# Three squared-ReLU feed-forwards of a two-block model: the next stage's input parts formed between the last evictions, squares folded on GpSimd, and a shorter interleave of column steps

## Chip, cores and metric

One core of a Trainium2 chip (trn2) runs the whole program. The metric is the device time of one execution in microseconds (us). Before the change the median of three runs is 1051.44 us (1051.43 to 1052.15). The engines are TensorE (PE; PEld is its weight load), VectorE (DVE), ScalarE (ACT), GpSimd (POOL) and SyncE (SP), which issues the weight transfers.

## The reference

256 tokens of width 1024 pass through two models in fp32. The first is a pooling and gated-delta-rule mixer followed by a feed-forward; the second is a spatial-gating mixer, a feed-forward, an RWKV-7 mixer and a feed-forward. What matters here is the feed-forward, which stands there three times (FFN1, FFN2, FFN3), and the norm in front of each stage:

```python
def rms_norm(x, w):
    return x * lax.rsqrt(jnp.mean(x * x, axis=-1, keepdims=True) + EPS) * w

h = h + jnp.square(jax.nn.relu(u @ w_up)) @ w_down      # u = rms_norm(h, norm_mlp), w_up 1024x4096, w_down 4096x1024
```

After FFN1 come the first model's final norm, the second model's first norm and the gating mixer (the kernel's `sgu` stage, whose first product is `h @ w_in`, 1024x4096). After FFN2 comes the RWKV mixer, whose first products are small low-rank ones. After FFN3 comes the final norm.

## The kernel before

**Layout.** The residual `x` stays in SBUF as 8 tiles of 128 channels by 256 tokens. Each fp32 matrix is multiplied as a high and a low part, both in the matmul's fast fp32r type. Weights come in 1 MB units (128x2048). SP loads a unit into one of four `raw` buffers, ACT copies it to `w_high` (`high`, L671), and DVE subtracts to get `w_low` (`low`, L1228). A load waits until the `low` of the unit four before it is done.

**Activations.** They are split in the same way: ACT writes `x` times the norm's channel weight to the high part, DVE writes the rest to the low part (L1493 before a feed-forward, L1520 `gating_low` before the gating stage, L1530 `mixer_low` before the RWKV stage). The norm's per-token factor is applied after the product. It needs the sum of squares of `x`: ACT squares all 8 tiles (L867), `halved` on DVE adds the tiles up in three steps of 1024, 512 and 256 columns (L1512, L1514), and one matmul with ones sums over channels (L2497).

**A feed-forward** (`mlp`) is 32 units m = 0 to 31, in four groups of 8: four units of `w_up`, then four of `w_down`. A unit is 16 column steps (2 tiles of 128 outputs by 8 slices k of the contraction), each of one 512-column matmul with the high weight (L2445) and one 256-column matmul with the low weight (L2446). Three pairs of PSUM banks are used in turn. An up unit is evicted by ACT (`copy_half`, L883), by a DVE add (L1550) and a DVE squared ReLU (L1556), and is then split by ACT (`hidden_high`, L889) and DVE (`hidden_low`, L1563). A down unit is evicted by ACT L883 and DVE L1550, L1570 and L1575, which adds it to two tiles of `x`. In each group the first two down units are interleaved, since their slices k = 6, 7 come from the fourth up unit: 12 column steps of unit m0+4, 12 of unit m0+5, then the 4 and 4 that are left. The last unit, m = 31, uses three 256-column matmuls a step (L2082 to L2084). Its first tile is released to DVE half a unit before its second (`last_tile`), and L1609 and L1611 add both to tiles 6 and 7 of `x`.

**Order around the change.** Each engine runs its list strictly in order, and the lists are written out by hand.

- On DVE, step m of the loop is: eviction of unit m, `low` of unit m+3, and `hidden_low` for an up unit. After the loop (m = 30) DVE runs `after_sum(0)` to `after_sum(2)`, that is the low parts of tiles 0 to 5 for the next stage, then L1609 and L1611 for tiles 6 and 7, then `after_sum(3)`. In FFN1 `after_sum` is `gating_low`, in FFN2 `mixer_low`, and in FFN3 nothing.
- On ACT the next stage's high parts (L909, L958), and its squares (L910, L960), stand behind the whole loop. In the RWKV stage `high` of unit `U_RKV+2` stands behind those.
- On PE the gating stage's first unit uses tiles 0 to 3 of the parts only, the second unit tiles 4 to 7. The RWKV stage starts with the sums over the squares of tiles 0 to 3, the small products of tile 0, the sums over tiles 4 to 7 (L2592), and the small products of tiles 1 to 7.
- GpSimd has little to do: three-step sums in the first mixer (L627, L630), a mask, and parts of the RWKV inputs (L644, L649).

## Time and profile before

| | |
|---|---|
| median of three runs | 1051.44 us (1051.43 to 1052.15) |
| the profiled execution | 1051.24 us, its span 1049.4 us |
| TensorE clock granted | 0.997 of full speed |
| PE busy | 1027.1 us (98%) |
| DVE busy | 823.9 us (79%) |
| ACT busy | 557.9 us (53%) |
| POOL busy | 32.6 us (3%) |
| DMA | 167 MB, 159 GB/s over the span |

The span is what the profile's rows cover; 1.8 us of the profiled execution's time lies around it. FFN1 runs from 127 to 308 us of the span, FFN2 from 459 to 639 us and FFN3 from 856 to 1039 us. A busy share is an average over the whole; what decides a stage is which wait of its bounding engine ends last there.

### The profile page before, as it was taken

Reading aid. Unit: us, or ns where it says so; the run is one execution under the profiler, and the core shown is the slowest. Engines: PE = TensorE matmul, PEld = TensorE weight load, DVE = VectorE, ACT = ScalarE, POOL = GpSimd, SP = SyncE. Lnnn points to the kernel's source line nnn. Section 1 sums busy time; section 2 is a strip of 40 time slices with the busy share of each in tenths; the row PEclk is TensorE's granted clock in tenths of the full one; section 3 lists DMA queues with packets and bytes.
Section 4 is the critical chain, followed back from the end, with each engine's and each line's share of the span. In section 5 each row is a group of like instructions: output and inputs, shape, how many; then the busy total and the mean of one; then the engine's idle time right before and its main releaser. Section 6 shows DMA issues by size and latency. Waiting matters only on the chain.

```text
span 1049.4 us, 17837 instructions
## 1 busy us (share of the span) xinstructions
PE 1027.1 (98%) x7496; PEld 928.3 (88%) x7496; DVE 823.9 (79%) x1176; ACT 557.9 (53%) x684; POOL 32.6 (3%) x39
## 2 busy tenths in 40 slices
PE   7999999999999999999999999999999999999997
PEld 7999988888887899998888888999898998888886
DVE  6989698687777787678979768799978667868775
ACT  6847554544536465355555446797553254544441
POOL 0004000000000000000000000042000000000000
PEclk9999999999999999999999999999999999999999
DMA  9722475565954755564656565414200157547531
GB/s 290 228 82 81 161 218 184 161 214 166 340 163 144 218 164 207 160 188 131 218 155 225 162 199 161 141 62 152 70 2 2 45 177 221 193 139 230 165 117 41
DMA packets 155936, 167.23 MB, mean 159 GB/s; under 512 B 5840, under 2 KB 148816, under 8 KB 155472
## 3 DMA queue, kind: packets, MB, share of 16 engines
q1 hardware_dynamic: 154672, 165.92, 49.9%
q8 instruction: 59, 0.97, 0.4%
q10 hardware_dynamic: 1184, 0.17, 0.2%
q14 instruction: 21, 0.17, 0.0%
HBM read 165.03 MB, written 1.05 MB: 158 GB/s over the span
## 4 chain that ended last, share of the span: by engine, by line
PE 79%; DVE 13%; ACT 3%; issue 2%; SPq 1%; DMA 1%; DVEq 0%; ACTq 0%
PE banks L2445 31%; PE banks L2446 16%; PE banks L2082 8%; PE banks L2084 7%; PE banks L2083 7%; DVE sb_w_low L1228 3%; DVE sb_arena L1915 1%; DVE sb_state L1912 1%; DMA sb_raw<-in_w_in 1%; ACT sb_w_high L671 1%; PE banks L2563 1%; SPq L550 1%; DVE sb_arena L1550 1%; PE banks L2696 0%; DVE sb_arena L1570 0%
## 5 line engine op out<-in xcount | busy, mean ns | idle before, releaser
L1228 DVE TENSOR_TENSOR sb_w_low<-sb_raw,sb_w_high 128x2048 fp32r<-128x2048 f32 x148 | 337.6, 2285 | 32.6 <-ACT sb_w_high L671 32.5
L671 ACT ACTIVATE sb_w_high<-sb_raw 128x2048 fp32r<-128x2048 f32 x148 | 281.8, 1908 | 12.3 <-PE banks L2084 10.2
L2445 PE MATMUL banks<-sb_act_parts,sb_w_high 128*128 128x512 f32 x768 | 270.6, 394 | 0.5 <-DVE sb_act_parts L1493 0.4
L2446 PE MATMUL banks<-sb_act_parts,sb_w_low 128*128 128x256 f32 x768 | 214.5, 279 | 0.0
L883 ACT ACTIVATE sb_arena<-banks 128x512 f32<-128x512 f32 x93 | 55.5, 597 | 243.7 <-PE banks L2446 243.7
L2445 PEld LDWEIGHTS banks<-sb_act_parts,sb_w_high 128*128 128x128 f32 x768 | 143.9, 187 | 36.1 <-DVE sb_act_parts L1493 0.7
L2082 PE MATMUL banks<-sb_act_parts,sb_w_low 128*128 128x256 f32 x584 | 169.3, 290 | 0.8 <-DVE sb_arena L1788 0.7
L2084 PE MATMUL banks<-sb_act_parts,sb_w_high 128*128 128x256 f32 x584 | 165.0, 282 | 0.0
L2083 PE MATMUL banks<-sb_act_parts,sb_w_high 128*128 128x256 f32 x584 | 164.0, 281 | 0.0
L1550 DVE TENSOR_TENSOR sb_arena<-sb_arena,banks 128x512 f32<-128x512 f32 x93 | 63.6, 684 | 102.4 <-ACT sb_arena L883 102.3
L2446 PEld LDWEIGHTS banks<-sb_act_parts,sb_w_low 128*128 128x128 f32 x768 | 144.0, 187 | 0.0
L2445 PE MATMUL banks<-sb_hidden_slots,sb_w_high 128*128 128x512 f32 x360 | 130.9, 395 | 1.3 <-DVE sb_hidden_slot L1563 1.3
L2445 PE MATMUL banks<-sb_hidden_slot,sb_w_high 128*128 128x512 f32 x360 | 130.2, 394 | 0.0
L2082 PEld LDWEIGHTS banks<-sb_act_parts,sb_w_low 128*128 128x128 f32 x584 | 109.9, 188 | 2.8 <-DVE sb_arena L1788 0.9
L2083 PEld LDWEIGHTS banks<-sb_act_parts,sb_w_high 128*128 128x128 f32 x584 | 110.7, 190 | 0.5 <-issue 0.2
L2084 PEld LDWEIGHTS banks<-sb_act_parts,sb_w_high 128*128 128x128 f32 x584 | 109.4, 187 | 0.0
L2446 PE MATMUL banks<-sb_hidden_slots,sb_w_low 128*128 128x256 f32 x360 | 100.9, 280 | 0.0
L2446 PE MATMUL banks<-sb_hidden_slot,sb_w_low 128*128 128x256 f32 x360 | 100.8, 280 | 0.0
L2445 PEld LDWEIGHTS banks<-sb_hidden_slots,sb_w_high 128*128 128x128 f32 x360 | 67.6, 188 | 18.6 <-DVE sb_w_low L1228 1.7
L2445 PEld LDWEIGHTS banks<-sb_hidden_slot,sb_w_high 128*128 128x128 f32 x360 | 67.5, 187 | 16.0
L2446 PEld LDWEIGHTS banks<-sb_hidden_slots,sb_w_low 128*128 128x128 f32 x360 | 67.5, 188 | 0.0
L2446 PEld LDWEIGHTS banks<-sb_hidden_slot,sb_w_low 128*128 128x128 f32 x360 | 67.5, 188 | 0.0
(469 smaller groups left out, 1530.7 us busy)
## 6 DMA issues: line engine op xcount, KB each, us to landing
sb_raw<-in_ffn_w SPq DMA_DIRECT2D x64, 1024.0 KB, 5.4
sb_raw<-in_w_up SPq DMA_DIRECT2D x16, 1024.0 KB, 5.5
sb_raw<-in_w_down SPq DMA_DIRECT2D x16, 1024.0 KB, 5.2
sb_raw<-in_sgu_w_in SPq DMA_DIRECT2D x16, 1024.0 KB, 5.6
sb_raw<-in_rwkv_w_rkv SPq DMA_DIRECT2D x12, 1024.0 KB, 5.2
sb_raw<-in_w_in SPq DMA_DIRECT2D x8, 1024.0 KB, 9.6
sb_raw<-in_sgu_w_out SPq DMA_DIRECT2D x8, 1024.0 KB, 5.0
sb_raw<-in_w_out SPq DMA_DIRECT2D x4, 1024.0 KB, 5.1
```

Of the source, the lines that this page charges most:

```text
L550: sp.dma_start(half_of(raw[j], t), w_in_v[:, :, c * 256 + t * P:c * 256 + t * P + P])\
L671: nc.scalar.activation(whi[s][:], raw[s][:], ACT.Copy).then_inc(hi_done, 1)
L883: nc.scalar.activation(dst, halves_at(FFN_BANK(m))[:, :, 1, :], ACT.Copy).then_inc(half_copied, 1)
L1228: nc.vector.tensor_tensor(wlo[s][:], raw[s][:], f32(whi[s][:]), ALU.subtract).then_inc(lo_done, 1)
L1550: nc.vector.tensor_tensor(t, t, halves_at(FFN_BANK(m))[:, :, 0, :], ALU.add).then_inc(unit_taken, 1)
L1912: base.add(nc.vector.tensor_tensor(tmp, RW.LB[:, j + 1:, j:j + 1].broadcast_to(shape), RW.WB[:, j:j + 1, 0:j + 1].broadcast_to(shape), ALU ...
L1915: base.add(nc.vector.tensor_tensor(RW.WB[:, j + 1:, 0:j + 1], RW.WB[:, j + 1:, 0:j + 1], tmp, ALU.add))
L2082: nc.tensor.matmul(dst, l_lo, r_hi, start=start, stop=False, **kw)
L2083: nc.tensor.matmul(dst, l_hi, r_lo, start=False, stop=False, **kw)
L2084: return nc.tensor.matmul(dst, l_hi, r_hi, start=False, stop=stop, **kw)
L2445: nc.tensor.matmul(two(dst), l_hi, parts, start=start, stop=False, skip_group_check=True)
L2446: return nc.tensor.matmul(dst[:, T:2 * T], l_lo, parts[:, 0, :], start=False, stop=stop, skip_group_check=True)
```

## The change

1. **GpSimd folds the squares.** `halved` on DVE is taken out of each feed-forward. A new function on GpSimd, `fold_squares`, does the same three additions and signals the same semaphore.
2. **The next stage's parts move into the loop.** On ACT `next_high(0)` stands behind `copy_half(29)`, `next_high(1)` behind `high` of step 29, `next_high(2)` and `(3)` behind step 30. On DVE `after_sum(0)` stands behind the eviction of unit 29. Behind the loop FFN1 has `after_sum(1)`, `(2)`, the last unit's tiles, `after_sum(3)`, and only then `low` of the gating stage's second unit (`u0+33`), which used to stand ahead of all of them. FFN2 has that `low`, the last tiles, and then `after_sum(1)` to `(3)`. In FFN2 ACT's `high(U_RKV+2)` stands ahead of the last two squares, and these are two operations of one tile each.
3. **Interleave.** Of the first two down units the order is now 12 steps of m0+4, 6 of m0+5, the last 4 of m0+4, 6 of m0+5, the last 4 of m0+5. For the fourth up unit of a group DVE runs `hidden_low` ahead of `low`.
4. **PE.** The RWKV stage's sums over tiles 4 and 5 stand ahead of the first small products. The gating stage's first matmul waits for `unit_taken`.

```diff
@@ -630,10 +630,22 @@
                     pool.wait_ge(box_sum, g + 1)
+        def fold_squares(j):
+            pool.wait_ge(sq_done, SQ[("ffn1", "ffn2", "ffn3")[j]] + 1)
+            for n in (4, 2):
+                chain.add(pool.tensor_tensor(FB.sq[:, 0:n, :], FB.sq[:, 0:n, :], FB.sq[:, n:2 * n, :], ALU.add))
+                chain.settle()
+            pool.tensor_tensor(FB.ss[j], FB.sq[:, 0, :], FB.sq[:, 1, :], ALU.add).then_inc(sq_folded, 1)
+        if on["ffn1"]:
+            fold_squares(0)
         if on["sgu"]:
...
             pool.memset(SG.ws[64:P, :, 0:64], 0.0).then_inc(mask_done, 1)
+        if on["ffn2"]:
+            fold_squares(1)
         if on["rwkv"]:
@@ -650,6 +662,8 @@
             pool.memset(RW.W6[0:32, :, 32:64], 0.0).then_inc(w_corner, 1)
+        if on["end"]:
+            fold_squares(2)
     @block.scalar
@@ -845,7 +859,7 @@
             high(U_OUT + 5)
-        def mlp(j):
+        def mlp(j, next_high=lambda c: None):
             u0, xd, h0 = FFN_U[j], FFN_X[j], FFN_H[j]
@@ -890,6 +904,8 @@
                 copy_half(m)
+                if m == len(FFN_ORDER) - 3:
+                    next_high(0)
                 if m + 4 < len(FFN_ORDER) or (m + 4 < len(FFN_ORDER) + 2 and u0 + m + 4 < n_units):
@@ -898,15 +914,42 @@
                     nc.scalar.activation(la_hi[n][:], RW.la_sc[n], ACT.Copy).then_inc(la_hi_done, 1)
+                if m == len(FFN_ORDER) - 3:
+                    next_high(1)
+            next_high(2)
+            next_high(3)
+        def gating_high(c):
+            act.wait_ge(g_done, 1)
+            act.wait_ge(x_done, X_FFN1 + c + 1)
+            for k in (2 * c, 2 * c + 1):
+                nc.scalar.activation(act_hi[:, k, :], x[:, k, :], ACT.Copy, scale=SG.g[:, k:k + 1]).then_inc(a_hi, 1)
+        def mixer_high(c):
+            def parts():
+                for k in (2 * c, 2 * c + 1):
+                    nc.scalar.activation(h_hi2[:, k, 1:T + 1], x[:, k, :], ACT.Copy, scale=vcol("norm_mix_g1", k))\
+                        .then_inc(a_hi, 1)
+            if c < 3:
+                act.wait_ge(x_done, X_FFN2 + c + 1)
+                parts()
+                nc.scalar.activation(RW.sq[:, 2 * c:2 * c + 2, :], x[:, 2 * c:2 * c + 2, :], ACT.Square)\
+                    .then_inc(sq_done, 1)
+                return
+            high(U_RKV + 2)
+            act.wait_ge(x_tile, 2)
+            nc.scalar.activation(RW.sq[:, 6, :], x[:, 6, :], ACT.Square)
+            act.wait_ge(x_done, X_FFN2 + 4)
+            nc.scalar.activation(RW.sq[:, 7, :], x[:, 7, :], ACT.Square).then_inc(sq_done, 1)
+            parts()
         if on["ffn1"]:
-            mlp(0)
+            mlp(0, gating_high if on["sgu"] else lambda c: None)
         if on["sgu"]:
-            act.wait_ge(g_done, 1)
-            for k in range(KT):
-                act.wait_ge(x_done, X_FFN1 + k // 2 + 1)
-                nc.scalar.activation(act_hi[:, k, :], x[:, k, :], ACT.Copy, scale=SG.g[:, k:k + 1]).then_inc(a_hi, 1)
             nc.scalar.activation(SG.sq[0][:], x[:], ACT.Square).then_inc(sq_done, 1)
@@ -950,15 +993,8 @@
         if on["ffn2"]:
-            mlp(1)
+            mlp(1, mixer_high if on["rwkv"] else lambda c: None)
         if on["rwkv"]:
-            for c in range(4):
-                act.wait_ge(x_done, X_FFN2 + c + 1)
-                for k in (2 * c, 2 * c + 1):
-                    nc.scalar.activation(h_hi2[:, k, 1:T + 1], x[:, k, :], ACT.Copy, scale=vcol("norm_mix_g1", k))\
-                        .then_inc(a_hi, 1)
-                nc.scalar.activation(RW.sq[:, 2 * c:2 * c + 2, :], x[:, 2 * c:2 * c + 2, :], ACT.Square).then_inc(sq_done, 1)
-            high(U_RKV + 2)
             act.wait_ge(ss_done, SS["rwkv"] + 1)
@@ -1534,8 +1570,6 @@
             low(u0 + 3)
-            dve.wait_ge(sq_done, SQ[("ffn1", "ffn2", "ffn3")[j]] + 1)
-            halved(FB.sq, FB.ss[j]).then_inc(sq_folded, 1)
             def token_scale():
@@ -1579,10 +1613,14 @@
                     down_taken(m)
-                u = u0 + m + 3
-                if m and (m + 3 < len(FFN_ORDER) or (m + 3 < len(FFN_ORDER) + 2 and u < n_units)):
-                    low(u)
-                if FFN_ORDER[m][0] == "up":
+                up_last = FFN_ORDER[m][0] == "up" and m % 8 == 3
+                if up_last:
+                    hidden_low(m)
+                if m == len(FFN_ORDER) - 3:
+                    after_sum(0)
+                if m and (m + 3 < len(FFN_ORDER) or (m + 3 == len(FFN_ORDER) and u0 + m + 3 < n_units)):
+                    low(u0 + m + 3)
+                if FFN_ORDER[m][0] == "up" and not up_last:
                     hidden_low(m)
@@ -1594,23 +1632,36 @@
                             .then_inc(la_lo_done, 1)
-            for c in range(3):
-                after_sum(c)
             t, b = FB.t[j][1], FFN_BANK(len(FFN_ORDER) - 1)
-            dve.wait_ge(x_added, 12 * j + 12)
-            dve.wait_ge(x_done, FFN_XO[j] + 2)
-            for i in range(2):
-                if i:
-                    dve.wait_ge(w_used, u0 + len(FFN_ORDER))
-                else:
-                    dve.wait_ge(last_tile, j + 1)
-                chain.add(nc.vector.tensor_tensor(t[:, i, :], tiles_at(b)[:, i, :], FB.r2[j], ALU.mult))
-                chain.settle()
-                nc.vector.tensor_tensor(x[:, 6 + i, :], x[:, 6 + i, :], t[:, i, :], ALU.add)\
-                    .then_inc(x_done if i else x_tile, 1)
-            after_sum(3)
+            def last_taken():
+                dve.wait_ge(x_added, 12 * j + 12)
+                dve.wait_ge(x_done, FFN_XO[j] + 2)
+                for i in range(2):
+                    if i:
+                        dve.wait_ge(w_used, u0 + len(FFN_ORDER))
+                    else:
+                        dve.wait_ge(last_tile, j + 1)
+                    chain.add(nc.vector.tensor_tensor(t[:, i, :], tiles_at(b)[:, i, :], FB.r2[j], ALU.mult))
+                    chain.settle()
+                    nc.vector.tensor_tensor(x[:, 6 + i, :], x[:, 6 + i, :], t[:, i, :], ALU.add)\
+                        .then_inc(x_done if i else x_tile, 1)
+            u = u0 + len(FFN_ORDER) + 1
+            if j == 1 and u < n_units:
+                low(u)
+                last_taken()
+                after_sum(1)
+                after_sum(2)
+                after_sum(3)
+            else:
+                after_sum(1)
+                after_sum(2)
+                last_taken()
+                after_sum(3)
+                if u < n_units:
+                    low(u)
         def scale_lora(n):
@@ -2468,17 +2519,16 @@
                 return FB.slots[k // 2][:, :, k % 2, :]
-            def down(m, ks=range(KT)):
+            def down(m, t, ks):
                 q = FFN_ORDER[m][1]
...
                 pe.wait_ge(h_lo, h0 + 4 * q + ks[-1] // 2 + 1)
-                for t in range(2):
-                    for k in ks:
-                        cs = slice(t * P, t * P + P)
-                        ins = wide(bank[FFN_BANK(m) + t], h[:, k, cs], l[:, k, cs], hidden_of(q, k),
-                                   start=k == 0, stop=k == KT - 1)
-                if ks[-1] == KT - 1:
-                    ins.then_inc(w_used, 1)
+                for k in ks:
+                    cs = slice(t * P, t * P + P)
+                    ins = wide(bank[FFN_BANK(m) + t], h[:, k, cs], l[:, k, cs], hidden_of(q, k), start=k == 0,
+                               stop=k == KT - 1)
+                return ins
             def down_last(m):
@@ -2495,13 +2545,19 @@
                     nc.tensor.matmul(bank[6][:, 0:T], ones, FB.ss[j], start=True, stop=True).then_inc(ss_done, 1)
-                down(m0 + 4, range(6))
-                down(m0 + 5, range(6))
-                down(m0 + 4, range(6, KT))
-                down(m0 + 5, range(6, KT))
-                down(m0 + 6)
+                down(m0 + 4, 0, range(6))
+                down(m0 + 4, 1, range(6))
+                down(m0 + 5, 0, range(6))
+                down(m0 + 4, 0, range(6, KT))
+                down(m0 + 4, 1, range(6, KT)).then_inc(w_used, 1)
+                down(m0 + 5, 1, range(6))
+                down(m0 + 5, 0, range(6, KT))
+                down(m0 + 5, 1, range(6, KT)).then_inc(w_used, 1)
+                down(m0 + 6, 0, range(KT))
+                down(m0 + 6, 1, range(KT)).then_inc(w_used, 1)
                 if m0 + 7 < len(FFN_ORDER) - 1:
-                    down(m0 + 7)
+                    down(m0 + 7, 0, range(KT))
+                    down(m0 + 7, 1, range(KT)).then_inc(w_used, 1)
                 else:
@@ -2540,6 +2596,8 @@
                         if g == 0 and m == 0:
+                            if k == 0:
+                                pe.wait_ge(unit_taken, 31)
                             pe.wait_ge(a_lo, A_SGU + k + 1)
@@ -2605,11 +2663,11 @@
             input_sums(1)
+            input_sums(2)
             pe.wait_ge(la_lo_done, 2)
...
             small_products(0)
-            input_sums(2)
             input_sums(3).then_inc(ss_done, 1)
...
```

## Rows read from the trace of the kernel before

**Rows 1.** The page's chain of work that ended last: shares of the span by engine.

```profile
PE 79%; DVE 13%; ACT 3%; issue 2%; SPq 1%; DMA 1%; DVEq 0%; ACTq 0%
```

**Rows 2.** Waits of PE: line, releaser, us in total, times, longest.

```profile
PE banks L2592 <- ACT sb_over_act L960: 2.4, 1, 2.4
...
PE banks L2082 <- DVE sb_act_parts L1520: 1.5, 1, 1.5
...
PE banks L2445 <- DVE sb_hidden_slot L1563: 1.3, 1, 1.3
```

**Rows 3.** FFN2 as one stretch: us, busy us of PE, PEld, DVE, ACT, POOL; clock, DMA.

```profile
458.70:639.50 180.80, 180.80 (x1045) 157.88 (x1044) 146.98 (x147) 95.23 (x94) 0.00 (x0) 1.00 0.58 181
```

**Rows 4.** Timeline, end of FFN1 (start, us, engine, line, operation, idle before).

```profile
307.49 0.28 PE L2084 MATMUL banks<-sb_hidden_slot,sb_w_high 128*128 128x256 f32 x1
...
309.31 0.47 PE L2082 MATMUL banks<-sb_w_high,sb_act_parts 128*128 128x512 f32 x1 [1.54 <-DVE sb_act_parts L1520]
...
306.48 2.28 DVE L1228 TENSOR_TENSOR sb_w_low<-sb_raw,sb_w_high 128x2048 fp32r<-128x2048 f32 x1
...
308.68 2.45 DVE L1520 SCALAR_TENSOR_TENSOR sb_act_parts<-sb_x,sb_gating_norms,sb_act_parts 128x256 fp32r<-128x256 f32 x6
...
312.30 0.42 DVE L1611 TENSOR_TENSOR sb_x<-sb_x,sb_arena 128x256 f32<-128x256 f32 x1
...
312.76 0.91 ACT L909 ACTIVATE sb_act_parts<-sb_x,sb_gating_norms 128x256 fp32r<-128x256 f32 x2 [5.25 <-DVE sb_x L1611]
```

**Rows 5.** Timeline, end of FFN2, sums and squares of the RWKV input.

```profile
639.37 1.89 PE L2592 MATMUL banks<-sb_over_act,sb_ones 128*128 128x256 f32 x8
...
642.61 1.03 PE L2592 MATMUL banks<-sb_over_act,sb_ones 128*128 128x256 f32 x4
...
646.04 1.18 PE L2592 MATMUL banks<-sb_over_act,sb_ones 128*128 128x256 f32 x4 [2.40 <-ACT sb_over_act L960]
...
638.25 2.29 DVE L1228 TENSOR_TENSOR sb_w_low<-sb_raw,sb_w_high 128x2048 fp32r<-128x2048 f32 x1
...
644.10 0.43 DVE L1611 TENSOR_TENSOR sb_x<-sb_x,sb_arena 128x256 f32<-128x256 f32 x1
...
645.37 0.61 ACT L960 ACTIVATE sb_over_act<-sb_x 128x512 f32<-128x512 f32 x1
```

**Rows 6.** Timeline, start of FFN3, to the first down unit.

```profile
862.30 1.90 ACT L867 ACTIVATE sb_arena<-sb_x 128x2048 f32<-128x2048 f32 x1
...
866.03 2.29 DVE L1228 TENSOR_TENSOR sb_w_low<-sb_raw,sb_w_high 128x2048 fp32r<-128x2048 f32 x1 [0.91 <-ACT sb_w_high L671]
...
868.24 1.94 DVE L1512 TENSOR_TENSOR sb_arena<-sb_arena 128x1024 f32<-128x1024 f32 x2
...
870.22 0.43 DVE L1514 TENSOR_TENSOR sb_arena<-sb_arena 128x256 f32<-128x256 f32 x1
...
880.93 0.68 DVE L1563 TENSOR_TENSOR sb_hidden_slot<-sb_arena,sb_hidden_slot 128x512 fp32r<-128x512 f32 x1
...
881.76 0.47 PE L2445 MATMUL banks<-sb_hidden_slots,sb_w_high 128*128 128x512 f32 x1 [1.29 <-DVE sb_hidden_slot L1563]
```

**Rows 7.** Timeline, the same place in FFN1: last hidden part, first down matmul.

```profile
149.34 0.69 DVE L1563 TENSOR_TENSOR sb_hidden_slot<-sb_arena,sb_hidden_slot 128x512 fp32r<-128x512 f32 x1
...
150.18 0.47 PE L2445 MATMUL banks<-sb_hidden_slots,sb_w_high 128*128 128x512 f32 x1
```

**Rows 8.** Timeline, GpSimd beside DVE in the first mixer.

```profile
82.83 2.28 DVE L1228 TENSOR_TENSOR sb_w_low<-sb_raw,sb_w_high 128x2048 fp32r<-128x2048 f32 x1
...
82.99 2.60 POOL L630 TENSOR_TENSOR sb_arena<-sb_arena 128x256 f32<-128x256 f32 x1 [44.13 <-DVE sb_arena L1279]
...
85.66 0.64 POOL L627 TENSOR_TENSOR sb_arena<-sb_arena 128x271 f32<-128x271 f32 x1
...
90.83 0.94 POOL L630 TENSOR_TENSOR sb_arena<-sb_arena 128x256 f32<-128x256 f32 x1
...
91.33 0.99 DVE L1447 TENSOR_TENSOR sb_keys_by_token<-sb_arena,sb_keys_by_token 128x512 f32<-128x512 f32 x1
```

## The prediction, made before the changed kernel was run

> **What bounds the kernel now.** I read the chain of work that ended last first: 79% of it is matmuls, 13% DVE [rows 1]. So only time in which PE stands still can be won. The list of what PE waited for comes next. Apart from the program's start it has three entries over 1 us, and each touches a feed-forward: squares from ACT (L2592), gating parts from DVE (L1520), a hidden part from DVE (L1563) [rows 2]. Third I read one feed-forward as a stretch: FFN2 takes 180.8 us, all of it PE-busy, with DVE busy 147.0 and ACT 95.2 [rows 3]. A unit is therefore 180.8/32 = 5.65 us and one of its 16 column steps about 0.35 us. Inside a feed-forward nothing is to be won on PE, but DVE has only about 1 us to spare per unit, which matters below. Last come the timelines around the three waits.
>
> End of FFN1 [rows 4]: PE's last matmul starts at 307.49 and its next at 309.31. Matmuls of this kind follow each other every 0.12 us, so 1.7 us is lost (the row's 1.54 counts from a modelled end). The cause is the order on DVE. The `low` of the second gating unit, which PE needs a whole unit later, runs from 306.48 to 308.76, and the low parts of tiles 0 to 5 only start at 308.68. PE's row starts as the first of them ends.
>
> End of FFN2 [rows 5]: PE does four sums from 639.37, the small products of tile 0, two more sums from 642.61, and then idles 2.40 us until the squares of tiles 6 and 7. DVE has again a `low` first (638.25 to 640.54), then the six low parts, and takes the last tile only at 644.53. ACT's two high parts stand ahead of its square (645.37 to 645.98). Four sums took 1.7 us (eight matmuls, 1.89 less the tail of the last), so two take 0.87. The loss from start to start is 646.04 - 642.61 - 0.87 = 2.6 us.
>
> Start of FFN3 [rows 6]: the first down unit waits 1.3 us (start to start 1.5) for `hidden_low` of the third up unit, 880.93 to 881.61. Before it DVE has hardly paused since the fold of the squares (868.24 to 870.65). In FFN1 the same part ends at 150.03 and PE starts at 150.18 [rows 7]: just in time, no loss.
>
> **The change part by part.**
>
> *FFN1's end.* The low parts of tiles 0 and 1 now come right behind unit 29, tiles 2 to 5 behind unit 30. Let E be the end of FFN1 on PE. Unit 28 ends at E - 14.7 (5.6 + 5.6 + 10 steps of 0.35), unit 29 at E - 11.2, unit 30 at E - 5.6. An eviction is ACT's copy (0.6, as a 128x512 operation [rows 5]) and three DVE operations (each about 0.7, as the hidden part [rows 6]). DVE's list from E - 13.9 on is: eviction (2.1), `low` (2.2), eviction of unit 29 (to E - 7.5), two low parts (0.8, from 2.45/6 each [rows 4]), `low` (to E - 4.5), eviction of unit 30 (to E - 2.4), four low parts (to about E - 0.9, the last two behind ACT). The gating stage's first unit uses tiles 0 to 3 alone, so PE goes on at once: -1.7 us. Its new wait, `unit_taken`, was met at about E - 3.8. What is late next is `low` of the second unit, which moved to the very end. From E DVE does L1609 and L1611 (0.85), waits for ACT's two high parts (0.9 [rows 4]; DVE's first starts halfway), does two low parts (ending about E + 2.4), then `low` (2.28): E + 4.7. PE needs it one unit after E: 24 matmuls of 512 columns, 0.23 each by the part of a column step beyond the 256-column one (0.35 - 0.12), so E + 5.6. It is covered with 0.9 us to spare; without that cover it would cost its own length, 2.3. Behind it in DVE's queue stand a fold of squares (2.4) and the third unit's `low` (2.3), done by E + 9.4 and needed at E + 11.2. On SP the load of the unit four later waits for the moved `low`, some 4 us later than now, and its `high` comes only after the first gating group: no cost.
>
> *FFN2's end.* By the same count unit 30 is evicted at E - 2.4. DVE does `low` of the second RKV unit until about E - 0.2 and takes the last two tiles by E + 1.4. ACT does two parts and a square (1.5), then `high` of the third RKV unit (1.9, as its 128x2048 square [rows 6]) until about E + 1.0, so the square of tile 7 (about 0.5) ends near E + 1.9. PE covers that with six sums (2.6) and the small products of tile 0 (642.61 - 639.37 - 1.73 = 1.5): it reaches the last sums at E + 4.1. The whole gap goes: -2.6 us; I count 2.5. The remaining low parts are done by E + 3.8, and PE needs tile 2 only after E + 5. The norm's factor is ready sooner as well, since ACT's `high` is no longer in front of it.
>
> *The fold on GpSimd.* DVE is rid of 2.4 us per feed-forward (1.94 and 0.43) [rows 6]. The same additions on GpSimd: one over 271 columns with no DVE operation of two SBUF inputs beside it takes 0.64 us [rows 8]; scaled to 1024 + 512 + 256 columns that is 4.3 us, less if part of the 0.64 is fixed. The sum is needed at 880, and the squares are ready at 864.20, so its own length is covered by 11 us. But GpSimd and DVE get in each other's way. A GpSimd addition of 256 columns that started beside `low` (82.83 to 85.11) ended at 85.59, 2.60 us instead of about 0.64. In turn a DVE operation of 128x512 (normally 0.69, as the hidden part) took 0.99 beside GpSimd [rows 8]. One waits while the other has the inputs.
>
> So in FFN3: GpSimd starts when `low` of unit 2 ends (about 865.1) and holds to about 867.4. `low` of unit 3, ready at 866.03, ends near 869.6 instead of 868.32. GpSimd's second addition holds to 870.7; the eviction's add reads PSUM and passes, but the squared ReLU waits and ends at 871.3 instead of 871.97. DVE is earlier by about 0.7 us and not by 2.4. The bounds are 1.5 (no hindrance: the whole stall goes) and -1.9 (every microsecond of the 4.3 held against DVE: 2.4 - 4.3). I take 0.8, near the walk-through. In FFN1 and FFN2 there is no stall to remove. DVE has there 0.1 us of margin at that point, and the same walk gives a DVE between equal and 1 us earlier: 0.
>
> The Trainium skill, SBUF — State Buffer, section "SBUF: two separate sides", states a lock between a GpSimd operation and a DVE operation with two SBUF inputs, held for the whole instruction. By that rule a 1024-column addition blocks `low` for all its length, as in my walk, and the sum stays; if short holds were shared instead, FFN3 would gain 1.5 and the sum 0.7 more. Rows 8 agree with the rule for 256 columns, and no row shows a longer addition on GpSimd.
>
> *Interleave.* The hidden part of the fourth up unit is now needed after 18 steps instead of 24: 6.3 us instead of 8.4 after that unit. It comes after copy, `high` and `hidden_high` on ACT (0.6 + 1.9 + 0.6, by the same rows) and 0.7 on DVE: 3.8 us. Margin 2.5; cost 0. `low` moved behind it ends at about 6.1 and is needed at 11.2. The first down unit finishes 6 steps (2.1 us) earlier, which spreads the evictions; PE wins nothing.
>
> *Sum.* -1.7 - 2.5 - 0.8 = -5.0 us. The profiled execution, 1051.24 with a span of 1049.4, would become 1046.2 with a span of 1044.4. It lies 0.2 below the median of the runs, so against the median I forecast 1046.4. Everything behind each gap waits on PE or on work released by it, and moves along.
>
> **The rivals.**
>
> - *The fold is free for DVE* (GpSimd alone waits): FFN3's 1.5 us go whole, 1051.44 - 5.7 = 1045.7. For it: `low` at 82.83 took its normal 2.28. Against it: the 0.99 of L1447.
> - *Gap 1 comes back one unit later*: if DVE is over 0.9 us later than I walked it, the moved `low` holds PE at the second gating unit. With 1.5 lost there: about 1047.9.
> - *The fold doesn't free DVE*: GpSimd blocks it for all 4.3 us. DVE is 1.9 later in each of three places with 0.1 us of margin, 1.8 + 1.8 + 1.9 = 5.5 against 1.7 + 2.5 won: 1052.7 at the worst, near 1051 with half of it hidden in DVE's pauses. The change then does nothing to be seen.
> - *Slower: GpSimd is slow for real.* If 2.60 us for 256 columns is its own pace and no waiting, the fold takes 7 times that, 18.2 us. PE's ones matmul then waits in each feed-forward. In FFN3, 864.2 + 18.2 = 882.4 and up to 2.3 for the `low` ahead of it, against a start at 880.3; in the other two it is about 3.5 late too. That is 3.5 + 3.5 + 4.4 - 1.5 (the stall that is there already) = about 10 lost against 4.2 won, near 1057. PE begins to wait once a fold takes over 14 us (880.3 - 864.2 - 2.3), and the change loses from about 15.5 us on. Against it: 0.64 us three microseconds later.
>
> **How the numbers follow.** Forecast 1046.4: chance 0.52. Free fold 1045.7: 0.22. Moved `low` 1047.9: 0.12. Fold doesn't free DVE: 0.08. Slow GpSimd: 0.06. What a measurement of this kernel can tell is about 0.2%, 2.1 us, so "faster" means below 1049.3. The first three cases are faster: 0.86. The fourth is mostly within: 0.07, the rest of it and the last case slower: 0.07. The range's low end takes the free fold and 0.8 us for a shorter RWKV start: 1044.8. The high end takes the moved `low` together with no gain in FFN3: 1048.9. That leaves out about 2 in 10.
>
> **What would show it.** PE's wait for L1520 and for ACT's square (L960) gone from its list; at FFN1's end the moved `low` ending about 4.7 us after PE's last FFN1 matmul; a wait of under 1 us left for the hidden part in FFN3; GpSimd additions of about 2.3, 1.2 and 0.6 us plus waiting, and a `low` of over 3 us beside the first. I am wrong if PE waits at the gating stage's second unit, if new waits on L1563 show up in FFN1 or FFN2, or if the ones matmul waits for GpSimd.

## The result, and the profile after

The changed kernel takes 1044.03 us (median of 4 runs, 1043.7 to 1044.1) where the kernel before takes 1051.43 beside it: a ratio of 0.9935 [0.992, 0.9951], which is 6.8 us less by the ratio and 7.4 us less by the medians. A second comparison gave 1044.34 (1044.27 to 1045.42, 5 runs) and 0.9933 [0.992, 0.9946]. The forecast was 1046.4 with a low end of 1044.8: the sign was right, but 5.0 us were forecast, some 2 us too few, and the result lies 0.8 us outside the range. The runs of one kernel lie in groups (26 runs of the kernel before: 5 at 1049.5 to 1049.9, 15 at 1050.8 to 1051.4, 6 at 1052.3 to 1053.4); what makes them is part of the answer below.

The page of the changed kernel, its chain of work that ended last (span 1042.2 us, execution 1044.1), answers to [rows 1]; the list of what PE waited for (line, releaser, us in total, times, longest) answers to [rows 2]; FFN2 as a stretch answers to [rows 3] (us; busy us of PE, PEld, DVE, ACT, POOL; granted clock; DMA).

```profile
PE 83%; DVE 11%; ACT 3%; issue 2%; SPq 1%; DMA 1%; DVEq 0%; ACTq 0%
```

```profile
PE banks L2242 <- DMA sb_x<-in_x_t: 5.5, 1, 5.5
PE banks L2133 <- DVE sb_arena L1839: 0.7, 1, 0.7
PE banks L2958 <- DVE sb_arena L1968: 0.6, 1, 0.6
PE banks L2496 <- DVE sb_hidden_slot L1597: 0.6, 1, 0.6
```

```profile
456.70:637.50 180.80, 180.80 (x1046) 158.09 (x1045) 149.11 (x150) 96.75 (x95) 7.01 (x3) 1.00 0.58 181
```

Apart from the program's start no wait over 0.7 us is left. The squares (2.4) and the gating parts (1.5) are gone, and the hidden part went from 1.3 to 0.6. FFN2 takes as long as before, to 0.2 us (180.8 us in both stretches).

The end of FFN1, which answers to [rows 4] (start, us, engine, line, operation, idle before):

```profile
307.28 0.28 PE L2135 MATMUL banks<-sb_hidden_slot,sb_w_high 128*128 128x256 f32 x1
...
307.40 0.40 PE L2133 MATMUL banks<-sb_w_high,sb_act_parts 128*128 128x512 f32 x1
...
309.19 0.88 DVE L1556 SCALAR_TENSOR_TENSOR sb_act_parts<-sb_x,sb_gating_norms,sb_act_parts 128x256 fp32r<-128x256 f32 x2 [0.71 <-ACT sb_act_parts L927]
...
309.99 2.28 DVE L1264 TENSOR_TENSOR sb_w_low<-sb_raw,sb_w_high 128x2048 fp32r<-128x2048 f32 x1
```

PE goes on after 0.12 us where it took 1.82 (start to start). The moved `low` ends at 312.27, which is 4.9 us after PE's start of 307.40.

The end of FFN2, which answers to [rows 5]:

```profile
637.16 2.75 PE L2650 MATMUL banks<-sb_over_act,sb_ones 128*128 128x256 f32 x12
...
638.61 0.42 ACT L946 ACTIVATE sb_over_act<-sb_x 128x256 f32<-128x256 f32 x1 [0.25 <-DVE sb_x L1648]
...
641.19 1.03 PE L2650 MATMUL banks<-sb_over_act,sb_ones 128*128 128x256 f32 x4
641.84 0.19 PEld L2133 LDWEIGHTS banks<-sb_mixer_input_high,sb_lora_low 128*128 128x128 f32 x1
641.87 0.47 PE L2133 MATMUL banks<-sb_mixer_input_high,sb_lora_low 128*128 128x256 f32 x1
```

The last square is done at 639.03, 2.2 us before PE wants it. From the first sum to the second tile's small products PE takes 4.71 us instead of 7.45 (646.82 - 639.37): -2.74.

The start of FFN3, which answers to [rows 6]:

```profile
857.57 6.42 POOL L637 TENSOR_TENSOR sb_arena<-sb_arena 128x1024 f32<-128x1024 f32 x2 [116.62 <-ACT sb_arena L881]
864.07 1.07 POOL L639 TENSOR_TENSOR sb_arena<-sb_arena 128x256 f32<-128x256 f32 x1
...
859.33 3.50 DVE L1264 TENSOR_TENSOR sb_w_low<-sb_raw,sb_w_high 128x2048 fp32r<-128x2048 f32 x1 [0.92 <-ACT sb_w_high L685]
...
863.46 1.07 DVE L1590 SCALAR_TENSOR_TENSOR sb_arena<-sb_arena 128x512 f32<-128x512 f32 x1
...
873.50 0.68 DVE L1597 TENSOR_TENSOR sb_hidden_slot<-sb_arena,sb_hidden_slot 128x512 fp32r<-128x512 f32 x1
...
874.33 0.48 PE L2496 MATMUL banks<-sb_hidden_slots,sb_w_high 128*128 128x512 f32 x1 [0.56 <-DVE sb_hidden_slot L1597]
```

The `low` beside GpSimd's first addition takes 3.50 us instead of 2.28 (the prediction walked 3.6), and PE's wait shrinks by 0.73 us start to start.

**Where the time went.** I compared when the same matmul (by its number in PE's list) starts in the two traces. Over the profiled pair the gain is 7.24 us at FFN3's last matmul: 0.21 by the end of FFN1, 1.70 at that end, 0.10 in the gating stage, 0.20 in FFN2, 2.74 at its end, **1.51 in the stretch of the RWKV stage from the second tile's small products to the decay product** (17.55 to 16.04 us), 0.25 in the rest of RWKV, 0.73 at FFN3's first down unit, less 0.20 given back behind it. The 1.51 is in none of my terms. The trace of before has its cause, in rows that I had not read. PE goes on at 646.04, behind the 2.40 us pause of [rows 5]. First its timeline a little later, then three stretches (same columns as above; the last but two is the granted clock):

```profile
647.65 0.41 PE L2082 MATMUL banks<-sb_mixer_input_high,sb_lora_low 128*128 128x256 f32 x1
647.86 0.41 PE L2083 MATMUL banks<-sb_mixer_input_low,sb_lora_high 128*128 128x256 f32 x1
...
650.79 0.28 PE L2083 MATMUL banks<-sb_mixer_input_low,sb_lora_high 128*128 128x256 f32 x1
650.90 0.28 PE L2084 MATMUL banks<-sb_mixer_input_high,sb_lora_high 128*128 128x256 f32 x1
```

```profile
646.04:647.00 0.96, 0.96 (x5) 0.86 (x5) 0.01 (x1) 0.96 (x1) 0.00 (x0) 1.00 1.10 350
646.80:650.40 3.60, 3.60 (x18) 3.57 (x17) 1.76 (x6) 3.54 (x6) 0.00 (x0) 0.53 1.10 349
650.50:654.10 3.60, 3.60 (x32) 3.60 (x31) 3.60 (x10) 3.60 (x8) 0.00 (x0) 1.00 0.21 66
```

and the same place in the changed kernel:

```profile
642.00:645.60 3.60, 3.60 (x32) 3.57 (x31) 2.37 (x7) 3.28 (x6) 0.00 (x0) 1.00 1.05 292
```

Behind the pause PE runs for 0.96 us more at the full clock (2.4 GHz), and then for about 3.4 us at the lower one (1.2 GHz): 16 matmuls of 256 columns start 0.213 us apart instead of 0.118, which costs 16 x 0.095 = 1.5 us. PE counts as fully busy in that time, so neither its busy share nor a list of waits shows it.

The Trainium skill, TensorE: Matmul & The Clock Gate, section "HAM oscillation — how this bites in real kernels", says that pauses between groups of matmuls let the clock fall, so that the next group starts at the lower one. The trace of before agrees that the clock falls behind a pause (0.53 against 1.00). It differs in two points, and there the trace decides: the fall comes 0.96 us after the next group has started, and the pause of 2.40 us is shorter than the waits for DMA in the page's example.

### The profile page after: what moved, and what is told of

It reads as the page before. It is cut to its first block, busy times and chain, and to the rows that moved or that the text cites. A ratio compares the mean times of both kernels' runs of the same rounds, so it can differ in the third digit from the quotient of the medians.

```text
span 1042.2 us, 17910 instructions
## 1 busy us (share of the span) xinstructions
PE 1025.3 (98%) x7496; PEld 927.8 (89%) x7496; DVE 824.7 (79%) x1167; ACT 558.9 (54%) x685; POOL 54.9 (5%) x48
## 4 chain that ended last, share of the span: by engine, by line
PE 83%; DVE 11%; ACT 3%; issue 2%; SPq 1%; DMA 1%; DVEq 0%; ACTq 0%
PE banks L2496 32%; PE banks L2497 16%; PE banks L2133 8%; PE banks L2135 8%; PE banks L2134 8%; DVE sb_w_low L1264 2%; DVE sb_arena L1966 1%; DVE sb_state L1963 1%; DMA sb_raw<-in_w_in 1%; ACT sb_w_high L685 1%; PE banks L2754 1%; PE banks L2621 1%; SPq L550 1%; PE banks L2865 0%; DVE sb_arena L1432 0%
## 5 line engine op out<-in xcount | busy, mean ns | idle before, releaser
L1264 DVE TENSOR_TENSOR sb_w_low<-sb_raw,sb_w_high 128x2048 fp32r<-128x2048 f32 x148 | 341.3, 2310 | 33.1 <-ACT sb_w_high L685 33.1
```

The costliest lines, as they stand in the source:

```text
L1264: nc.vector.tensor_tensor(wlo[s][:], raw[s][:], f32(whi[s][:]), ALU.subtract).then_inc(lo_done, 1)
```

## The experiments

**1. Is the missing 1.5 us the clock?** To the kernel before I add five ones matmuls, whose result nobody uses, in the pause. The last sums still wait for the same square.

```diff
             input_sums(2)
+            for _ in range(5):
+                nc.tensor.matmul(bank[7][:, 0:T], ones, RW.sq[:, 0, :], start=True, stop=True)
             input_sums(3).then_inc(ss_done, 1)
```

> The kernel before with five more ones matmuls into an unused bank between the sums over tiles 4 and 5 and the last sums, so PE is busy for 2.15 of the 2.6 us that it otherwise stands still; what it waits for comes no sooner. The results of these matmuls are not used. Theory (the pause drops the clock): the half clock is gone and 1.5 us are won although the wait's end stays. Rival (the rest of the gain at this place comes from the norm's factor and ACT's high being earlier): no change, within 0.2 us.

Measured: 1049.62 us (1049.17 to 1051.01, 10 runs), 0.9988 [0.9979, 0.9997]. PE's timeline:

```profile
644.37 2.32 PE L2614 MATMUL banks<-sb_over_act,sb_ones 128*128 128x256 f32 x10
646.92 1.13 PE L2592 MATMUL banks<-sb_over_act,sb_ones 128*128 128x256 f32 x4 [0.24 <-ACT sb_over_act L960]
```

```profile
646.90:650.50 3.60, 3.58 (x26) 3.47 (x27) 1.01 (x5) 3.55 (x4) 0.00 (x0) 1.00 1.10 346
```

The square comes no sooner, yet the stretch from the first sum to the decay product takes 23.50 us instead of 25.00. With PE kept busy the clock stays at 1.00 and the 1.5 us come back. So they hang on PE standing still, and come on top of the time for which it does.

**2. Does the pause always cost them?** Two ways: the kernel before once more, unchanged, and the changed kernel with a pause of the old size put back (11 squares of tile 7 that are not needed, ahead of the real one).

> The kernel before once more, for a second profile. Its timed runs lie in groups near 1049.6, 1051.1 and 1052.5 us. Theory: two things vary from execution to execution, the start (FFN1's first matmul at 127 or at 128.5 us) and the half clock behind the pause at FFN2's end (3.4 us of it or none), each worth 1.3 to 1.5 us; the profile shows which two this execution had, and they add up to its time. Rival: the groups come from elsewhere, and the stretch from FFN2's end to the decay products is 25.0 us as before without a half clock.

```diff
             act.wait_ge(x_done, X_FFN2 + 4)
+            for _ in range(11):
+                chain.add(nc.scalar.activation(RW.sq[:, 7, :], x[:, 7, :], ACT.Square))
+                chain.settle()
             nc.scalar.activation(RW.sq[:, 7, :], x[:, 7, :], ACT.Square).then_inc(sq_done, 1)
```

> The changed kernel with 11 needless squares of tile 7 on ACT ahead of the one that PE waits for, each about 0.47 us: PE stands still again for about 2 to 3 us at FFN2's end. Theory (a pause of this length drops the clock): the half clock comes back for 3.4 us behind the pause, and the stretch from FFN2's end to the RWKV stage's decay products is longer by the pause plus 1.5 us. Rival (the half clock of before had another cause): longer by the pause alone.

> The kernel with the late square once more, for a second profile. In its first profile PE stood still for 2.8 us and the clock stayed at full speed, though the timed runs lie at 1047.2 once, at 1048.5 to 1048.9 six times and at 1049.8 to 1050.1 three times. Theory (such a pause drops the clock in most executions, not in all): this profile shows either no half clock and about 1047.1 us, or 3.4 us of half clock behind the pause and about 1048.6 us. Rival (the pause has nothing to do with it): no half clock whatever the time; the 1.4 us between the groups then lie at the start alone.

Measured: before again 1049.91 us in its profiled execution, with the same 2.40 us wait and no drop; the stretch takes 23.50 us. Changed with the pause: 1048.73 us (1047.15 to 1050.13, 10 runs), 0.9981 [0.9972, 0.999]. Its profiled execution (1047.15) has no drop, a second one (1050.05) has. The stretch behind the pause in before again, then behind a pause of 2.67 and of 2.66 us in the other two:

```profile
646.80:650.40 3.60, 3.60 (x31) 3.55 (x30) 1.59 (x6) 3.54 (x5) 0.00 (x0) 1.00 1.10 352
```

```profile
645.00:648.40 3.40, 3.40 (x30) 3.38 (x29) 2.59 (x9) 2.96 (x5) 0.00 (x0) 1.00 1.10 348
```

```profile
646.80:650.20 3.40, 3.40 (x18) 3.40 (x17) 2.59 (x9) 3.34 (x7) 0.00 (x0) 0.50 1.10 349
```

The same pause costs 1.5 us in one execution and nothing in the next. The 1050.05 is made up of 1047.15, a start of FFN1 that is 1.3 us later, and 1.5 for the clock. The same pause stands in the traces of experiments 4 and 7 (FFN1's end alone, the fold alone), and both have the drop: four traces of six with the pause in all. This also explains the groups: FFN1's first matmul starts at 126.9 to 127.5 us in eight traces and at 128.0 to 128.7 in the other eight, whatever the kernel, and a run with the pause may or may not have the drop.

The mean granted clock that is listed for each run tells how often. In the 16 traces it is 0.997 or less where the drop is there and 0.998 or more where it is not. Of the kernel before's 26 runs 20 have 0.997 or less. The other six are the whole lowest group and one run of the middle group (1051.02), which fits a late start without the drop. In its four comparisons together the kernel before has the drop in 42 of 57 runs, the changed kernel with the pause in 9 of 11. The 38 runs of kernels without the pause and the ten with the filled one all have 0.998 or 0.999. The seven faster runs of the filled kernel (1049.17 to 1049.79) lie where the kernel before's lowest group does. The changed kernel has only the groups of the start (1044.3 and 1045.4 in its second comparison).

**3. FFN2's end alone** (the kernel before, with the parts of the change that touch it):

```diff
+            if j == 1:
+                low(u0 + len(FFN_ORDER) + 1)
+                last_taken()
+                after_sum(1)
...
+            input_sums(2)
...
             small_products(0)
-            input_sums(2)
             input_sums(3).then_inc(ss_done, 1)
```

> The kernel before with only FFN2's end changed (parts and squares in the loop, ACT's high of the third RKV unit ahead of the last two squares, the sums over tiles 4 and 5 ahead of the small products). Theory: this edit takes away PE's 2.40 us wait and with it the 3.4 us at half clock (1.2 GHz instead of 2.4) that the trace of before shows right behind that wait, in which 16 matmuls ran at 0.213 us each instead of 0.118: 2.7 + 1.5 = about 4.2 us won. Rival, the prediction's own term: the wait alone, 2.5 to 2.7 us won, and the rest of the 7.4 us comes from elsewhere.

Measured: 1048.16 (1047.06 to 1048.62, 5 runs), 0.9968 [0.9955, 0.9981]. Between the first sum and the decay product the profiled execution gains 2.61 + 1.51 = 4.12 us, with no drop of the clock:

```profile
644.40:648.00 3.60, 3.60 (x28) 3.43 (x27) 3.33 (x10) 3.12 (x7) 0.00 (x0) 1.00 1.06 297
```

The 4.2 stands; a gain of the pause alone falls. In a run of the kernel before that has no drop, only the 2.6 are there to be won.

**4. FFN1's end alone:**

```diff
+            if j == 0:
+                after_sum(1)
+                after_sum(2)
+                last_taken()
+                after_sum(3)
+                low(u0 + len(FFN_ORDER) + 1)
```

> The kernel before with only FFN1's end changed. Theory: 1.7 us won, the distance of the two matmuls beyond their step; no half clock there before, so nothing beyond it. Rival: part of the unexplained 2.4 us is here (the gating stage's folds start earlier against PE), 2.5 us or more won.

Measured: 1050.52 (1048.91 to 1051.89, 10 runs), 0.9995 [0.9986, 1.0004]: no gain clear of the noise. The trace has the 1.70 us won at the first gating matmul and 1.19 lost behind it, nearly all one unit later, so 0.5 is left. DVE's parts and `low`, then PE at the gating stage's second unit:

```profile
311.06 0.88 DVE L1529 SCALAR_TENSOR_TENSOR sb_act_parts<-sb_x,sb_gating_norms,sb_act_parts 128x256 fp32r<-128x256 f32 x2 [0.71 <-ACT sb_act_parts L913]
311.86 2.28 DVE L1237 TENSOR_TENSOR sb_w_low<-sb_raw,sb_w_high 128x2048 fp32r<-128x2048 f32 x1
314.20 0.50 PE L2104 MATMUL banks<-sb_w_high,sb_act_parts 128*128 128x512 f32 x1 [1.00 <-DVE sb_w_low L1237]
```

DVE is 1.9 us later here than in the changed kernel (311.86 against 309.99, at the same start of the gating stage). Theory and rival of the expectation both missed this: the part depends on another one.

**5. Which one? The changed kernel with the old interleave:**

```diff
                 down(m0 + 5, 0, range(6))
+                down(m0 + 5, 1, range(6))
                 down(m0 + 4, 0, range(6, KT))
                 down(m0 + 4, 1, range(6, KT)).then_inc(w_used, 1)
-                down(m0 + 5, 1, range(6))
```

> The changed kernel with the old interleave of the first two down units (12, 12, 4 and 4 column steps). Theory, from the run with FFN1's end alone: unit 28 ends 2.1 us later, DVE's row of evictions, parts and lows at FFN1's end moves back by about 1.3 us, and PE waits 1.2 us for the moved low at the gating stage's second unit; nothing elsewhere. Rival, the prediction's own term: the interleave costs and gains nothing, 0.

Measured: 1047.0 (1045.73 to 1047.63, 6 runs), 0.9964 [0.9951, 0.9976]. The wait is back, 1.15 us at the gating stage's second unit. The rest of the profiled execution loses another 0.3 us in small steps. DVE's row and PE's:

```profile
313.59 2.28 DVE L1264 TENSOR_TENSOR sb_w_low<-sb_raw,sb_w_high 128x2048 fp32r<-128x2048 f32 x1
315.93 0.50 PE L2133 MATMUL banks<-sb_w_high,sb_act_parts 128*128 128x512 f32 x1 [1.00 <-DVE sb_w_low L1264]
```

The interleave releases unit 28 six steps sooner, DVE's row at FFN1's end moves up, and the moved `low` comes in time. It is worth 1.2 us at this place, beside the moved `low`. The interleave without the other parts was not run, so its worth alone is not shown. This run keeps `hidden_low` ahead of `low` for the fourth up unit; that half of part 3 was not run apart either.

**6. FFN1 with FFN2's order on DVE** (`low` ahead of the last tiles and of `after_sum(1)`):

```diff
-            if j == 1 and u < n_units:
+            if j < 2 and u < n_units:
                 low(u)
```

> The changed kernel, in FFN1 with FFN2's order on DVE behind the loop: low of the next stage's second unit and the last tiles ahead of the low parts of tiles 2 to 7. Theory (PE's first gating unit needs tiles 2 and 3 four to six steps in): DVE is done with the last tiles at about 1.4 us after FFN1's end, tile 2's part is ready at 1.9 and PE asks for it at 1.4, so about 0.5 us is lost and no more. Rival (the low at the end is what PE waits for in the changed kernel): some gain.

Measured: 1044.94 (1044.67 to 1046.17, 4 runs), 0.995 [0.9935, 0.9964]. By the trace PE loses 0.43 us where it first needs tile 2, and 0.10 at the second unit. The order that was chosen is the better one.

**7. The fold alone, and the change without it.** In the first, `halved` gives way to `fold_squares` in the kernel before; in the second it comes back in the changed one:

```diff
             low(u0 + 3)
+            dve.wait_ge(sq_done, SQ[("ffn1", "ffn2", "ffn3")[j]] + 1)
+            halved(FB.sq, FB.ss[j]).then_inc(sq_folded, 1)
```

> The kernel before with only the fold moved to GpSimd. Theory (one engine waits for the other's whole instruction): the wait for the hidden part in FFN3 falls from 1.3 to about 0.6 us, 0.7 us won, and a low beside the first addition takes 3.5 us. Rival (the fold is free for DVE): 1.5 us won.

> The changed kernel with the fold of the squares back on DVE. Theory: 0.7 to 0.8 us lost in FFN3, where the wait for the hidden part is 1.3 us again instead of 0.6, nothing in FFN1 and FFN2. Rival (the fold's move is worth more through the later units): over 1.5 us lost.

Measured: 1049.87 (1048.31 to 1051.74, 10 runs), 0.9983 [0.9972, 0.9994], with 0.74 us won at FFN3's first down unit; and 1045.67 (1045.18 to 1046.78, 4 runs), 0.9956 [0.9941, 0.9971], with 0.73 lost there, 0.19 in FFN1, 0.17 in FFN2 and 0.24 in the RWKV stage. Within the change the fold is worth about 1.3 us; with the old interleave FFN1 and FFN2 kept nothing of it.

The 0.24 in the RWKV stage is no noise. In every trace with the fold on DVE, DVE pauses 0.3 us in front of the same addition without waiting for anything that the profile shows, and in no trace with the fold on GpSimd. The first line is of the kernel before, the second of the changed one:

```profile
804.95 1.29 DVE L1927 TENSOR_TENSOR sb_raw<-banks,sb_constants 128x512 f32<-128x512 f32 x2 [0.30 <-issue]
798.09 1.29 DVE L1978 TENSOR_TENSOR sb_raw<-banks,sb_constants 128x512 f32<-128x512 f32 x2
```

Why the shorter list of DVE lacks this pause is open.

**8. The rest of FFN3's wait.** Either GpSimd's hold is made shorter, by folding in additions of 256 columns, or `hidden_low` of a group's third up unit goes ahead of `low`, as the fourth's already does. Both start from the changed kernel:

```diff
-                chain.add(pool.tensor_tensor(FB.sq[:, 0:n, :], FB.sq[:, 0:n, :], FB.sq[:, n:2 * n, :], ALU.add))
+                for k in range(n):
+                    chain.add(pool.tensor_tensor(FB.sq[:, k, :], FB.sq[:, k, :], FB.sq[:, n + k, :], ALU.add))
```

> The changed kernel with the fold on GpSimd in seven additions of 256 columns instead of three of 1024, 512 and 256. Theory (one engine waits for the other's whole instruction): a low beside it waits for one short addition, 0.5 us instead of 1.2, and the wait for the hidden part in FFN3 falls from 0.6 to about 0.1 to 0.3 us; the fold itself takes longer, since it gets in only between DVE's operations. Rival (what counts is the total time that both need): the wait in FFN3 stays at 0.6 us.

```diff
-                up_last = FFN_ORDER[m][0] == "up" and m % 8 == 3
+                up_last = FFN_ORDER[m][0] == "up" and m % 8 in (2, 3)
```

> The changed kernel with hidden_low ahead of low for the third up unit of a group as well as for the fourth. Theory (in FFN3 PE waits for that hidden part, and only DVE's order makes it late): it comes 1.5 us sooner, the wait of 0.6 us (0.8 from start to start) is gone, 0.8 us won against the changed kernel, and 0.1 to 0.2 us in FFN1 and FFN2. Rival (the low that now comes later is late in turn, or the hidden part of the fourth unit is): no gain, a new wait for L1264 or L1597 two units on.

> The changed kernel once more, in more runs. Its first four all lay at 1043.7 to 1044.1. Theory (only the start varies, since no pause is left that drops the clock): groups near 1044.0 and 1045.3 us, none 1.5 us above these without a later start, and a median between 1044.0 and 1045.3, 6 to 7 us under the kernel before. Rival (the changed kernel's start is sooner by the change): all runs at 1044.0 again.

> The kernel with hidden_low ahead of low for the third up unit as well, once more beside the changed kernel on the same chip. Theory: each of its groups lies 0.7 us under the changed kernel's (near 1043.3 and 1044.6). Rival: no difference, the 0.7 us that its trace shows in FFN3 is given back later.

Measured in pieces (one execution, 1044.86, with the late start): PE's wait is 0.18 us, which is within the forecast of 0.1 to 0.3. By the end of FFN3 0.43 us is won against the changed kernel, about half of what the next edit wins there. DVE and GpSimd:

```profile
858.85 7.42 POOL L638 TENSOR_TENSOR sb_arena<-sb_arena 128x256 f32<-128x256 f32 x6 [116.68 <-ACT sb_arena L882]
...
860.61 2.53 DVE L1265 TENSOR_TENSOR sb_w_low<-sb_raw,sb_w_high 128x2048 fp32r<-128x2048 f32 x1 [0.92 <-ACT sb_w_high L686]
...
865.68 1.14 DVE L1598 TENSOR_TENSOR sb_hidden_slots<-sb_arena,sb_hidden_slots 128x512 fp32r<-128x512 f32 x1 [0.70 <-ACT sb_hidden_slots L904]
```

`low` is held 0.25 us instead of 1.22, but the fold is still running when the first hidden part is due, and that takes 1.14 instead of 0.69. PE's first down matmul:

```profile
875.22 0.47 PE L2497 MATMUL banks<-sb_hidden_slots,sb_w_high 128*128 128x512 f32 x1 [0.18 <-DVE sb_hidden_slot L1598]
```

With the third hidden part first the wait is gone. DVE's row, and PE without a pause in front of the first down matmul:

```profile
873.47 0.69 DVE L1597 TENSOR_TENSOR sb_hidden_slot<-sb_arena,sb_hidden_slot 128x512 fp32r<-128x512 f32 x1 [0.70 <-ACT sb_hidden_slot L903]
874.08 2.28 DVE L1264 TENSOR_TENSOR sb_w_low<-sb_raw,sb_w_high 128x2048 fp32r<-128x2048 f32 x1
```

```profile
874.57 0.59 PE L2547 MATMUL banks<-sb_arena,sb_ones 128*128 128x256 f32 x2
874.81 0.59 PE L2496 MATMUL banks<-sb_hidden_slots,sb_w_high 128*128 128x512 f32 x1
```

It measured 1044.02 (1043.4 to 1045.45, 4 runs), 0.9936 [0.9917, 0.9954], with both groups of the start in it. Beside the changed kernel in one comparison (1044.34, 1044.27 to 1045.42, 0.9933 [0.992, 0.9946]) it takes 1043.4 (1043.25 to 1044.7, 5 runs), 0.9925 [0.991, 0.994]: 0.9 us less by the medians. Both traces give about 0.8 of it in FFN3 (0.9 at the first down unit, 0.1 given back behind it). The second trace gains 0.35 more in the RWKV stage, which the first does not, so this is not put down to the edit. It is the fastest version here, though the intervals of the two ratios overlap widely.

## Why the prediction was off, point by point

- **FFN1's end, -1.7: held, for a reason half told.** PE goes on at once. The moved `low` ended at E + 4.9 where I walked E + 4.7. But this rests on the new interleave, which I had costed at 0: the walk put unit 28 at the new order's E - 14.7 without saying that the old one would cost something. Without it (experiments 4 and 5) the part is worth 0.5. The rival of the moved `low` (1.5 lost) didn't come in the changed kernel; its mechanism came, with 1.2, in both runs that have the moved `low` and the old interleave.
- **FFN2's end, -2.5: 2.74 by the trace.** The square of tile 7 was done at E + 2.0 (walked: 1.9), and PE came for it at E + 4.1 as walked, E being 637.05.
- **The clock: the step that failed.** The term for FFN2's end was "The whole gap goes: -2.6 us; I count 2.5". It priced the pause and stopped at its end, and so put what lies behind the pause at nothing without a reason. In the profiled execution, and in most runs of the kernel before, the pause had a tail, 16 matmuls at half the clock, worth 1.5 us. The edit at FFN2's end alone won 4.12 us, not 2.5. I had the granted clock of the whole span, 0.997, and of FFN2, 1.00, and never read it for the 4 us behind the pause, where it is 0.53. The mean hides it: 3.4 us at half the clock in 1049 make 0.998. The low end of the range took the free fold and 0.8 us for a shorter start of RWKV, which is the place but not the cause, and half the size. By their own terms the ends come to 1044.9 and 1048.7 (1051.44 - 1.7 - 2.5 + 1.5), not 1044.8 and 1048.9; the result lies outside either way.
- **The fold, -0.8 in FFN3: 0.73, and 0.74 by itself.** The walk was right: `low` 3.50 us (3.6 walked), squared ReLU 1.07 instead of 0.69. The three additions take 3.1, 3.2 and 1.07 us with their waiting. Taking off the time until the DVE operation in front has ended, about 2.3, 1.2 and 0.6 remain, the scaled sizes. The free fold (1.5) falls, since `low` is held. The fold that doesn't free DVE falls, and slow GpSimd too: done at 865.14, wanted at 873.17.
- **The fold in FFN1 and FFN2, 0.** In the kernel before it gave nothing that stayed there, as said. Under the new interleave, taking it back cost 0.19 and 0.17: again two parts that are worth more together. The 0.24 that it wins in the RWKV stage was in none of the terms.
- **The sum.** 1.70 + 2.74 + 1.51 + 0.73 = 6.7 us against the 5.0 forecast, and 6.8 to 7.4 measured. The 0.56 that is left of the profiled pair's 7.24 is spread over five places. The 0.25 in the rest of RWKV comes with the fold, as said. The 0.21 by the end of FFN1 is no more than what executions of one kernel differ by there (0.20 and 0.39 in two pairs). The sum has its clock term from one execution with the drop; in the medians that term counts in full only because most runs of the kernel before have it.

The Trainium skill, SBUF — State Buffer, section "SBUF: two separate sides", has the lock held for the whole instruction. The hold of 1.22 us under a 1024-column addition and of 0.25 us under 256-column ones agree with it.

**What stays open.** Why the same pause lowers the clock in one execution and not in another was seen and not settled; in the four traces with the drop it begins between 0.14 us before and 1.31 us after PE goes on. Nor is it settled why the first mixer ends some 1.2 us later in half of the traces (PE's wait for a DVE result there is 1.5 us in all eight of these and at most 0.7 in the others). Behind the shorter pause at FFN1's end in the kernel before (1.54 us, [rows 4]) the granted clock stayed at 1.00, by the stretch that follows it; no pause between that and 2.4 us was tried, so no length from which a pause costs extra is shown.

```profile
309.30:312.90 3.60, 3.59 (x15) 2.91 (x16) 3.36 (x9) 0.14 (x1) 0.00 (x0) 1.00 0.82 253
```

## What to carry to other kernels

Read the granted clock in the few microseconds behind every pause of TensorE, not as a mean over the span: a pause that goes may take a tail of its own with it. Cost parts of a change together where one moves an engine's row and another lives on the slack in it: the interleave was costed at 0 and was worth 1.2 us with the moved `low`. Where the time between two groups of runs equals a cost in the trace, compare executions of one kernel before explaining the difference of two.

## What the runs showed of the hardware

- Around the end of a pause of 2.4 to 2.7 us of TensorE the granted clock fell to half for 3.4 us in some executions and not in others of the same kernel (0.53 and 1.00; 0.50 and 1.00), by the mean clocks in 42 of 57 runs of the kernel before. Five small matmuls in the pause kept it at 1.00 in the profiled execution, with 0.24 us of it left idle, and all ten runs have a mean of 0.998 or 0.999.
- GpSimd and VectorE wait for each other by whole instructions: a 128x2048 subtraction took 3.50 and 4.02 us beside a 1024-column addition on GpSimd, and 2.53 beside 256-column ones. Splitting removes about half of the loss and moves the rest on: the fold grew from 7.6 to 8.6 us, a later DVE operation took 1.14 us instead of 0.69, and 0.43 of the 0.83 us came back.
- Executions of one program reach FFN1 about 1.3 us apart (127.1 and 128.4 us in two of the same kernel), more than the last edit (0.9 us) is worth, so such a difference can be read only from several runs of both kernels side by side.
